# The odd mixer of a decoder step as one program: all convolution channels on TensorE in four column groups, and the modulation of layer 1 computed inside the products of layer 0

## What is computed

```python
mod = silu(c) @ ada_w[l] + ada_b[l]          # per layer l, for 9 conditioning rows; 6 * 1024 columns
sh1, sc1, g1, sh2, sc2, g2 = split(mod, 6)

def odd_mixer(h, ...):                       # layer 1
    u, a, gt = split(h @ w_in, [512, 1024])
    # pooling: causal window means of 2, 4, 8, 16 rows over u (one window per 128 channels), minus u,
    # then a 128x128 product per window group and a scale
    glu_ext = concat([conv_hist, a * sigmoid(gt)])           # 30 rows of history
    cv = depthwise_conv(glu_ext, conv_w) + conv_b            # 31 taps, 512 channels
    conv_out = silu(layer_norm(cv) * ln_g + ln_b)
    return concat([pool_out, conv_out]) @ w_out, last 15 rows of u, last 30 rows of glu
```

## Time and profile before

| | us |
|---|---|
| median of 3 runs | 3447.33 (3441.67 to 3450.09) |
| the profiled execution | 3445.84 |
| its span in the trace | 3444.1 |
| TensorE busy in it | 3095.5 (90%) |
| odd mixer, three blocks, from 2232.8 to 2476.0 | 243.2 |

### The profile page before, as it was taken

How to read it: one execution, slowest core, us unless ns; L and a number is a source line. 1 busy time by engine, 2 the same in 40 slices (tenths; PEclk the granted TensorE clock), 3 DMA queues, 4 the chain that set the end, 5 groups by cost and what they waited for, 6 DMA issues and landing times. The chain is left out here.

```text
span 3444.1 us, 45149 instructions
## 1 busy us (share of the span) xinstructions
PE 3095.5 (90%) x17877; PEld 2776.2 (81%) x17877; DVE 1291.0 (37%) x2017; ACT 1012.0 (29%) x1528; POOL 628.9 (18%) x368
## 2 busy tenths in 40 slices
PE   4799999888876988999999997979697999999997
PEld 3798899633332988999999987957397999999997
DVE  4155660366422173222222263069217222222225
ACT  3233432366432242212222132223223121222221
POOL 1211101111111212111221121162111222112210
PEclk7899999899998989999999999989698999999998
DMA  5322222100264221111111131030511111111112
GB/s 218 112 86 81 87 81 74 52 1 1 77 201 145 83 77 49 38 36 49 49 49 36 37 128 51 28 104 7 167 55 60 49 49 43 31 48 49 49 38 104
DMA packets 236584, 239.12 MB, mean 69 GB/s; under 512 B 7619, under 2 KB 194423, under 8 KB 236181
## 3 DMA queue, kind: packets, MB, share of 16 engines
q1 hardware_dynamic: 221317, 205.72, 19.0%
q0 software_dynamic: 5120, 16.78, 1.5%
q10 hardware_dynamic: 10016, 14.78, 1.2%
HBM read 207.74 MB, written 29.99 MB: 69 GB/s over the span
## 5 line engine op out<-in xcount | busy, mean ns | idle before, releaser
L614 PE MATMUL PS<-trunk_x_hi,trunk_w_hi 128*128 128x364 f32 x2208 | 740.3, 335 | 88.3 <-POOL trunk_w_lo L738 32.4
L615 PE MATMUL PS<-trunk_x_lo,trunk_w_hi 128*128 128x364 f32 x2208 | 737.3, 334 | 0.0
L616 PE MATMUL PS<-trunk_x_hi,trunk_w_lo 128*128 128x364 f32 x2208 | 735.3, 333 | 0.0
L746 POOL TENSOR_TENSOR trunk_w_lo<-trunk_w_raw,trunk_w_hi 128x1024 fp32r<-128x1024 f32 x128 | 307.0, 2398 | 1320.0 <-ACT trunk_w_hi L924 1229.7
L614 PE MATMUL PS<-hidden,trunk_w_hi 128*128 128x364 f32 x1536 | 507.9, 331 | 0.0
L615 PE MATMUL PS<-hidden,trunk_w_hi 128*128 128x364 f32 x1536 | 505.9, 329 | 0.0
L616 PE MATMUL PS<-hidden,trunk_w_lo 128*128 128x364 f32 x1536 | 505.5, 329 | 0.0
L614 PEld LDWEIGHTS PS<-trunk_x_hi,trunk_w_hi 128*128 128x128 f32 x2208 | 424.2, 192 | 90.4 <-POOL trunk_w_lo L738 33.3
L615 PEld LDWEIGHTS PS<-trunk_x_lo,trunk_w_hi 128*128 128x128 f32 x2208 | 424.5, 192 | 0.0
L616 PEld LDWEIGHTS PS<-trunk_x_hi,trunk_w_lo 128*128 128x128 f32 x2208 | 423.7, 192 | 0.0
L1175 DVE TENSOR_TENSOR M<-M,PS 128x364 f32<-128x364 f32 x336 | 178.4, 533 | 440.9 <-PE PS L616 440.9
(11 more groups left out here) (378 smaller groups left out, 3892.6 us busy)
## 6 DMA issues: line engine op xcount, KB each, us to landing
trunk_w_raw<-mlp_w SPq DMA_DIRECT2D x128, 512.0 KB
rec_ada_w<-ada_w SPq DMA_DIRECT2D x24, 1024.0 KB, 5.1
spare<-cache_sb_k SPq DMA_DIRECT2D x64, 256.0 KB, 3.2
values<-cache_sb_v POOLq DMA_DIRECT2D x64, 256.0 KB, 3.6
rec_w_raw<-even_w_in SPq DMA_DIRECT2D x28, 512.0 KB
x_scratch<-x_new ACTq DMA_DIRECT2D x9, 1456.0 KB, 5.9
x_new<-x_scratch SPq DMA_DIRECT2D x6, 1456.0 KB, 13.0
trunk_x_old<-x_scratch SPq DMA_DIRECT2D x6, 1456.0 KB, 9.9
```

What stands on the lines that cost most here:

```text
L614: pe.matmul(out, hi, xh, start=first, stop=False)
L615: pe.matmul(out, hi, xl, start=False, stop=False)
L616: return pe.matmul(out, lo, xh, start=False, stop=last)
L746: pool.tensor_tensor(wl[:, u % 4, :], raw[:, u % 2, :], wh[:, u % 4, :].bitcast(F32), ALU.subtract).then_inc(s_lo, 1)
```

## The change

Three parts.

1. The three blocks of the odd mixer become one, `odd_mixer`. All four channel blocks of the convolution go to TensorE in plain float32. For each 32 channels (column group b) the contraction of 128 rows holds four taps of 32 channels: S4 keeps four copies of the input, shifted by 0 to 3 rows, written by 16 DMAs from SBUF to SBUF per channel block (two slots, so block k from 2 on waits for the convolution of k - 2). The weights `taps` are 128x32 and are made on POOL from the turned tap rows and the constant `fold`; the tap rows come by eight small DMAs with 128-byte runs. 31 taps are NG = 8 groups. The glu goes straight into G (DVE), the copies into U go from POOL to ACT, the window means and the sum of squares go from POOL to DVE. The mean over channels is taken part by part between the convolutions.
2. The modulation of layer 1 leaves the odd mixer. Chunks 4 and 5 go to `recurrence` (14 chunks, 28 bursts, one turn after the last tile). Chunks 6 to 11 go to the loop of trunk0, one per group: `load_mod` puts four DMAs of 512 KB per group in the SP queue, with one slot; `modulation` puts a burst of two matmuls after each of phases 1 to 4 and a turn in phase 5; ACT copies the rows; DVE adds the bias; DVE zeroes PSUM bank 6 once before group 1, for which TensorE waits.
3. The coefficients of layer 1 are made by DVE inside the odd mixer.

The diff, its core (removed bodies of the three old blocks are left out; the kernel's functions above show them):

```diff
+            def load_mod(g, b):
+                sp.wait_ge(s_am, g * 4 + (b - 3))
+                sp.dma_start(wa[:, :, :], ada_v[:, 2 * b:2 * b + 2, bass.ds(g * (4 * P) + CH0 * 4 * P, 4 * P)])\
+                  .then_inc(s_wa, 16)
+
+            def load_group(g, mod=False):
                 for u in range(8):
+                    if mod and u == 2:
+                        load_mod(g, 0)
+                    if mod and u == 6:
+                        load_mod(g, 1)
                     sp.wait_ge(s_lo, g * 8 + (8 + u - 1))
...
+                if mod:
+                    load_mod(g, 2)
+                    load_mod(g, 3)
...
+            load_group(0)
+            with sp.Fori(1, G - 1) as g:
+                load_group(g, with_mod)
+            load_group(G - 1)
...
+            def mod_burst(g, b):
+                pe.wait_ge(s_wa, g * 64 + 16 * (b - 3))
+                for i in range(2):
+                    k = 2 * b + i
+                    q = pe.matmul(PS[CG * (k % 4):CG * (k % 4) + SEG, 6, :], core.cT[:, k, 0:SEG], wa[:, i, :],
+                                  start=(k < 4), stop=(k >= 4), skip_group_check=True)
+                q.then_inc(s_am, 1)
+
+            def mod_turn(g):
+                pe.wait_ge(s_ar, g)
+                pe.wait_ge(s_as, g)
+                for f in range(4):
+                    q = pe.matmul(PS[:, 7, f * SEGP:f * SEGP + SEG], mod_rows[:, f * P:(f + 1) * P], cols(core, "sel"),
+                                  start=True, stop=True)
+                q.then_inc(s_at, 1)
+
+            def modulation(g, phase, s):
+                if not with_mod:
+                    return
+                if phase in (1, 2, 3, 4) and s == 7:
+                    mod_burst(g, phase - 1)
+                if phase == 5 and s == 4:
+                    mod_turn(g)
+
...
+            if with_mod:
+                pe.wait_ge(s_az, 1)
...
+                    hidden_phase(g, c, False, lambda s: modulation(g, c, s))
...
+                    down_phase(g, c, lambda s: modulation(g, 3 + c, s))
...
+            if with_mod:
+                pe.wait_ge(s_as, G - 1)
...
+            with act.Fori(1, G - 1) as g:
                 for u in range(4):
                     high_weights_of_group(g, u)
                 rest_of_group(g)
+                if with_mod:
+                    act.wait_ge(s_am, g * 4 + 1)
+                    act.activation(mod_rows[:, :], PS[:, 6, :], ACT.Copy).then_inc(s_ar, 1)
+            for u in range(4):
+                high_weights_of_group(G - 1, u)
+            rest_of_group(G - 1)
...
+            if with_mod:
+                dve.memset(PS[:, 6, :], 0.0).then_inc(s_az, 1)
+                dve.sem_inc(s_as, 1)
             with dve.Fori(1, G - 1) as g:
...
+                if with_mod:
+                    dve.wait_ge(s_at, g)
+                    dve.tensor_tensor(core.mod[:, l + 1, :].rearrange("p (f c) -> p f c", c=SEGP)[:, bass.ds(g * 4 + 4 * CH0, 4), 0:SEG],
...
-    CHUNKS = [(0, c) for c in range(4, 12)] + [(1, c) for c in range(4)]
+    CHUNKS = [(0, c) for c in range(4, 12)] + [(1, c) for c in range(6)]
...
                         mod_burst(n)
+            mod_turn(NCH - 1)
...
+            mod_add(NCH - 1)
...
+            sp.dma_start(hp[:, :], core.state_pool.rearrange("o b t f -> (o b t) f")).then_inc(s_hi, 16)
+            sp.wait_ge(s_tz, 1)
+            for g in range(NG):
+                n = min(4, CWID - 4 * g)
+                sp.dma_start(tap_rows[16 * g:16 * g + 16, 0:n * CG].rearrange("b (s c) -> b s c", c=CG),
+                             core.conv_w[0, 4 * g:4 * g + n, :].rearrange("s (b c) -> b s c", c=CG)).then_inc(s_tr, 16)
+            sp.dma_start(pw[:, :, :], core.pool_w.rearrange("o g c d -> c (o g) d")).then_inc(s_pw, 16)
+            for k in range(NPE):
+                sp.wait_ge(s_G, k + 1)
+                if k >= 2:
+                    sp.wait_ge(s_cm, k - 1)
+                else:
+                    sp.wait_ge(s_z, 1)
+                for b in range(4):
+                    for s in range(4):
+                        sp.dma_start(S4[CG * s:CG * s + CG, k % 2, b, 0:GX - s], G[CG * b:CG * b + CG, k, s:GX])\
+                          .then_inc(s_sh[k], 16)
...
+            def conv(k):
+                pe.wait_ge(s_sh[k], 16 * 16)
+                pe.wait_ge(s_tp, k + 1)
+                if k == 0:
+                    pe.wait_ge(s_hl, HT)
+                    pe.wait_ge(s_tc, 1)
+                    pe.wait_ge(s_rc, 4)
+                if k >= 2:
+                    pe.wait_ge(s_cv, k - 1)
+                for g in range(NG):
+                    fl = dict(start=(g == 0), stop=(g == NG - 1), skip_group_check=True)
+                    for h in range(2):
+                        for b in range(4):
+                            pe.matmul(PS[CG * b:CG * b + CG, 2 * (k % 2) + h, :], taps[:, k, g, b, :],
+                                      S4[:, k % 2, b, 4 * g + 512 * h:4 * g + 512 * h + 512], **fl)
+                    for b in range(4):
+                        x = S4[:, k % 2, b, CHI + SEQ:].rearrange("p (s t) -> p s t", s=NSEQ)[:, :, 4 * g:4 * g + TQ]
+                        q = pe.matmul(PS[CG * b:CG * b + CG, 4 + k % 2, 0:NS].rearrange("p (s t) -> p s t", s=NSEQ),
+                                      taps[:, k, g, b, :], x, **fl)
+                q.then_inc(s_cm, 1)
...
+            def mean_part(k):
+                pe.wait_ge(s_cv, k + 1)
+                fl = dict(start=(k == 0), stop=(k == HT - 1), skip_group_check=True)
+                for h in range(2):
+                    pe.matmul(PS[:, 6 + h, :], cols(core, "ones").to_broadcast([P, P]), cv[:, k, h * 512:(h + 1) * 512], **fl)
+
+            def mean_tails():
+                pe.wait_ge(s_cz, 1)
+                for k in range(HT):
+                    q = pe.matmul(PS[:, 5, 256:256 + TP - SEQ], cols(core, "ones").to_broadcast([P, P]), cv[:, k, SEQ:TP],
+                                  start=(k == 0), stop=(k == HT - 1), skip_group_check=True)
+                q.then_inc(s_mu, 1)
...
+            def pool_product(g):
+                if g == 0:
+                    pe.wait_ge(s_pw, 16)
+                pe.wait_ge(s_pp, g + 1)
+                if g >= 2:
+                    pe.wait_ge(s_po, g - 1)
+                if g == 1:
+                    pe.wait_ge(s_muc, 1)
+                for h in range(2):
+                    pe.matmul(PS[:, 2 * (g % 2) + h, :], pw[:, g, :], Ut[:, g, h * 512:(h + 1) * 512], start=True, stop=True)
+                pe.matmul(PS[:, 4 + g % 2, 0:NS], pw[:, g, :], Ut[:, g, SEQ:T], start=True, stop=True).then_inc(s_pm, 1)
...
+            for k in range(NPE):
+                conv(k)
+                if k >= 1:
+                    mean_part(k - 1)
+            mean_part(NPE - 1)
+            mean_tails()
+            for g in range(HT):
+                pool_product(g)
+            pe.wait_ge(s_sa, HT - 1)
+            pe.wait_ge(s_po, HT)
+            column_sums(pe, core, 6, SUMS, sq[:, 0, :], True).then_inc(s_ss, 1)
+            pe.wait_ge(s_r, 1)
+            spread(pe, core, 3, r).then_inc(s_bc, 1)
...
+                act.activation(cv[:, k, 0:SEQ], PS[:, 2 * (k % 2):2 * (k % 2) + 2, :].rearrange("p b c -> p (b c)"),
+                               ACT.Identity, bias=b)
+                act.activation(cv[:, k, SEQ:T], PS[:, 4 + k % 2, 0:NS], ACT.Identity, bias=b).then_inc(s_cv, 1)
             act.wait_ge(s_mu, 1)
-            act.activation(chunked(mu[:, :]), PS[:, 0:NC3, 0:CW], ACT.Copy, scale=1.0 / HALF).then_inc(s_muc, 1)
+            act.activation(mu[:, 0:SEQ].rearrange("p (b c) -> p b c", b=2), PS[:, 6:8, :], ACT.Copy, scale=1.0 / HALF)
+            act.activation(mu[:, SEQ:TP], PS[:, 5, 256:256 + TP - SEQ], ACT.Copy, scale=1.0 / HALF).then_inc(s_muc, 1)
...
+            for g in range(HT):
+                act.wait_ge(s_pm, g + 1)
...
+            def glu(k):
+                gx = tail(G, k)
+                for h in range(2):
+                    dve.tensor_copy(gx[:, 4 * h:4 * h + 4, 0:CHI], PS[:, h, k * P:k * P + 4 * CHI].rearrange("p (s t) -> p s t", s=4))
+                dve.wait_ge(s_sg, k + 1)
+                dve.tensor_tensor(A_[:, k, SEQ:T], A_[:, k, SEQ:T], cv[:, k, SEQ:T], ALU.mult).then_inc(s_gs, 1)
+                dve.tensor_tensor(G[:, k, CHI:CHI + SEQ], A_[:, k, 0:SEQ], cv[:, k, 0:SEQ], ALU.mult)
+                dve.wait_ge(s_gs, k + 1)
+                dve.tensor_copy(gx[:, :, CHI:], samples(A_[:, k, :])).then_inc(s_G, 1)
...
+            dve.memset(G[:, :, 0:CHI], 0.0)
+            dve.memset(U[:, :, 0:PH], 0.0)
+            dve.memset(S4[:, :, :, GX - 4:GX], 0.0).then_inc(s_z, 1)
+            dve.wait_ge(s_hT, 2)
+            for k in range(HT):
+                glu(k)
+            dve.wait_ge(s_tT, 1)
+            dve.tensor_copy(tap_cols[:, :], PS[:, 3, 0:P]).then_inc(s_tc, 1)
+            dve.wait_ge(s_hT, 3)
+            for k in range(HT):
```

(24 more changed lines are left out.)

368 lines of the change are left out of this document (114 added, 254 removed).

## The result

The changed kernel takes 3373.77 us (median; 3365.0 to 3375.52), before 3446.18 us: ratio 0.9784, 95% interval 0.9771 to 0.9798, 72.4 us less. The forecast was 3375.5 with a range of 3358 to 3420. The profiled execution is the shortest of the four, 3365.0 us (span 3363.4), so its own difference is larger, 80.7 us of span.

| stage | before, us | after, us | difference | forecast |
|---|---|---|---|---|
| recurrence (first dense product to next block) | 531.05 | 537.84 | +6.8 | +8.9 |
| attention, until trunk0's first dense product | 483.56 | 478.53 | -5.0 | 0 |
| trunk0, until the odd mixer | 1114.36 | 1147.81 | +33.45 | +34.9 |
| odd mixer | 243.2 | 129.0 | -114.2 | -114.1 |
| trunk1 to the end | 968.1 | 966.3 | -1.8 | 0 |

What follows compares the result with a forecast made beforehand. The prediction took DVE's taps and chains of small steps to bound the odd mixer, and TensorE, without slack, trunk0. Terms -114.1, +34.9 and +8.9 sum to -70.3, from 3445.84 to 3375.5 us; range 3358 to 3420.

Steps and rivals of the forecast that it cites:

- Part B: Recurrence: two more modulation chunks, with four bursts, a turn and a longer tail, add 8.9 us, range 6 to 12.
- Part C: Odd mixer: one block with the convolution on TensorE takes 129.1 us in place of 243.2, a change of -114.1.
- Part A: Trunk0: the modulation's 24 bursts, 6 turns and a bank wait add 34.9 us, range 28 to 45.
- the bank's wait: Trunk0: TensorE waits once for DVE's last addition of group 0 and the zeroing of bank 6, about 1.3 us.
- the small round: Odd mixer's convolution: a tap group's round of 64-column products takes 0.3 us, between 0.107 of streaming and 0.50.
- the cold start: Start of the odd mixer's convolution: steps take double for about 4 us, adding 2.0 us.
- pooling step: Odd mixer's tail: ACT takes the pooling products after the squares, the third and fourth waiting for their product; 6.7 us.
- Rival 1: Odd mixer: shift copies at 100 GB/s, 27.8 us a block, set the pace; +43 us, 3419; chance 0.14.
- Rival 2: Odd mixer's convolution: weight loads are not hidden with four groups of 32 columns; +38 us, 3414; chance 0.05.
- Rival 3: Odd mixer's convolution: column groups run one after the other; +175 us, 3550; chance 0.04.
- Rival 4: Odd mixer's convolution: the clock stays at 1.2 GHz; +64 us, 3440, no difference; chance 0.04.
- Rival 5: Trunk0: a cover for the loads is too thin, 3 us lost per group; +18 us, 3394; chance 0.05.

Runs made afterwards that it cites:

- e1: The changed kernel with the modulation left out of trunk0 (no loads, bursts or turns there); 3334.2 us, ratio 0.9678 to the kernel before.
- e2: The changed kernel with a chunk's eight products in two bursts of four, each in four column groups, in place of four bursts of two; 3357.47 us, ratio 0.9743.
- e4: The changed kernel with every shift copy followed by a second one of the same size to a scratch tensor in DRAM; 3421.95 us.
- e3: The changed kernel with a channel block's 16 shift copies reordered, so four in succession read and write four different quarters of the partitions; 3372.59 us.
- e11: e7 with its loads' source dimensions exchanged, 32 rows outermost, then the four shifts, over the same 128 partitions; 3366.54 us.
- e5: The changed kernel without the 64-column products in six of eight tap groups of every channel block; 3364.45 us.
- e7: The changed kernel with shifted copies made through DRAM: one store per channel block, four loads over 128 partitions, outermost dimension four; 3441.11 us.
- e6: The changed kernel with the loops over 512-column halves and column groups exchanged, so one group's two products follow each other; 3375.58 us.
- e9: The changed kernel with bursts of four, earlier glu products, a reordered tail, the first block's copies in column halves and ten useless tail products; 3354.21 us.
- e10: The changed kernel with bursts of four, diagonal copy order, earlier glu products, a reordered tail and useless products in TensorE's three waits; 3343.36 us, ratio 0.9712.

## Why the prediction held

The total fits better than its parts: 3375.5 for 3373.8 is within 2 us, while Part B has a spread of 9 us from run to run and Part C hit its sum by errors of both signs. So near a hit is luck; the size of Part A and that of the odd mixer's gain are not.

**Part A** was right in size and in its reason. A burst is 1.16 (taken 1.17), a group 101.54 (101.6), the bank's wait 1.5 (1.3); 33.6 by e1 for 34.9, with 34.7 by the measured terms. The step "two products cost what four cost" was an argument from the earlier trace rows, and e2 shows it.

**Part B.** The end of recurrence answers to the earlier trace rows: the last eviction starts at 636.25, the rows are copied at 636.62, turned at 637.27, and the next block's TensorE starts at 641.71: 5.5 us where 2.0 were, 3.5 more (3.3). The whole stage was 6.8 longer, within 6 to 12. Its size isn't settled by single profiles, so that it fell within the range is in part luck: the same code has from 535.5 us (e2) to 544.6 (e4) in the twelve profiles of it, 535.7 in e1 and 543.3 in e3, where the granted clock between 110 and 300 us is 0.99 and 0.95. The kernel before has one profile, 531.05.

**Part C** was right in its sum, 129.0 for 129.1, through errors that cancelled: start +1.0, convolution -4.0, tail +3.0. The start came 25.2 after the block's start (24.2), from copies at about 200 GB/s. The 199 GB/s of the earlier trace rows were the right number for another reason than the nearest size, and that is luck: in that row the engines are only 0.64 busy, while in the changed kernel's copies they are full and 32 partitions hold them to 213 (e11). The convolution with its three mean parts, 2293.24 to 2360.8, took 67.6 where the sum has 71.6. The term that failed is the small round: 0.3 was taken between 0.107 and 0.50, and it is 0.11 (e5), 32 x 0.19 = 6.1 too much; the cold start cost 2.9 in place of 2.0, the mean parts are 1.9. The tail, from there to the next block, took 36.3 where the sum has 33.3. In this profile its pooling step was under-sized: from the end of the squares to the last pooled block are 9.5 us (2370.8 to 2380.3) where 6.7 was the term, since the third product waits for ACT and then runs at half clock. In e1, where the clock rose again during that product (3.24 us, the column sums after it 2.07), the same code's tail is 33.3, and the odd mixer 124.2. Of nine profiles with this tail three have 36.3 (the changed kernel, e2, e7) and six 33.3 to 33.9. So about 3 us of it, and 1.5 of the convolution's start, turn on when TensorE's clock falls and rises in a given run.

**Rival 1** had the right price, shown by e4. **Rival 2** falls: 0.86 a round and 0.11 for a small one are the streaming alone. The Trainium skill says in TensorE: Matmul & The Clock Gate, "Part 3: Packing small matmuls", that weight loads overlap only products in other row groups; here all use all 128 rows, and the trace doesn't agree: the weight loads are busy for 24.2 us of the convolution's 65.7, and none of it adds to the streaming. The same part also names a background weight buffer; whether that is what hides them no run here shows. **Rival 3** falls by the 1.71 us for eight products, in either order (e6). **Rival 4** falls by clock 1.00 from the third tap group on; 0.96 over the whole convolution. **Rival 5** falls by e1.

## What to carry to other kernels

Count a packed burst by its longest product and fill all four column groups: a half-filled burst costs the same. Let a transfer between partitions span all 128 with its outermost dimension large. Before splitting transfers for an earlier start, count the issues: what the queue needs for each is paid by every transfer behind them (e9 lost 4.8 us at the second block). In a chain of small steps, look in the queue for what stands ahead of the step that ends last, and at the granted clock after each wait: both gave more here than any single instruction.

## What the runs showed of the hardware that was not expected

- Copies of 32 partitions hold the DMA engines full at 201 to 232 GB/s (up to 255 in the order of e3); copies over 128 partitions reach 316 to 413 (e11). SP needs 0.6 us to issue a copy of 32 partitions (e9), and 0.8 in the changed kernel, where the earlier trace rows has 0.35 for small ones.
- The same bytes with an outermost dimension of four moved at 93 GB/s with a quarter of the DMA engines' time, with one of 32 at full share (e7, e11): 75 us of the kernel. The Trainium skill has it in DMA: Bandwidth & Descriptors, "Rules for kernel authors".
- Products of the same column group in succession don't hold up the other groups (e6): a channel block with its mean part takes 16.8 and 16.7 us in the two orders.
- Products without use in a wait pay when they end in time: column sums and spreading together fell from 9.24 to 4.98 us, and the first tap groups ran at full rate. What the work runs over has to be taken off: 0.9 us at the start in e10, 3.0 in the tail of e9.
- The same code can differ by 9 us in recurrence (535.5 to 544.6) and by 5 in the odd mixer (124.2 in e1, 129.0) from run to run, and the granted clock goes with it; a single profile is no measure of a part below that.
